# Dilated attention: tokens ordered by class mod 4, eight blocks a head in equal halves

## What is computed

```python
DIL_GROUPS = ((128, 1), (512, 4), (2048, 16))     # (window, dilation r)
# query t attends t - j*r, j = 0..window/r
s = einsum(q_g, k_g) * 64 ** -0.5                 # masked outside that window
m = max(s); p = exp(s - m); den = sum(p)
o_g = (p @ v_g) / den;  lse_g = m + log(den)
o = sum over g of softmax(lse)_g * o_g            # then o @ w_o, added to x
```

## Time and profile before

| | before |
|---|---|
| median of 3 runs | 2204.69 us (2204.66 to 2206.47) |
| the profiled execution | 2205.75 us |
| its span | 2203.9 us |
| TensorE busy | 2168.8 us, 98% |
| VectorE busy | 1475.0 us, 67% |
| ScalarE busy | 1196.1 us, 54% |
| GpSimd busy | 217.0 us, 10% |
| dilated stage, from its first product to the end of y | about 1719 to 2021 us of the span |
| between the last product of n = 8 and the first of y | 1934.9 to 1998.8 us |

### The profile page before, as it was taken

One profiled execution on the slowest core, in us unless ns is written; L12 is line 12 of the kernel. 1 busy time (PEld: TensorE's weight loads), 2 busy tenths in 40 slices (PEclk: granted clock), 3 DMA queues, 4 the chain that ended last, 5 costly groups with the idle time before them and its releaser, 6 DMA issues.

```text
span 2203.9 us, 29727 instructions
## 1 busy us (share of the span) xinstructions
PE 2168.8 (98%) x11759; PEld 1837.7 (83%) x11759; DVE 1475.0 (67%) x2097; ACT 1196.1 (54%) x1814; POOL 217.0 (10%) x228
## 2 busy tenths in 40 slices
PE   9999999999999999999999999998999999999999
PEld 9878888997888878888877888777888888877887
DVE  7645755897666767667745755686655699685665
ACT  5555544756445645455555544566544566475443
POOL 0000100472000011000000200002000100051000
PEclk9999999999999999999999999999999999999999
DMA  8534656523655535655544655551655566513653
GB/s 267 187 134 153 203 192 191 163 77 120 208 190 165 174 115 190 192 191 173 185 145 160 172 190 194 182 173 58 206 191 191 182 173 187 172 39 102 201 191 119
DMA packets 201817, 368.95 MB, mean 167 GB/s; under 512 B 6991, under 2 KB 142543, under 8 KB 201680
## 3 DMA queue, kind: packets, MB, share of 16 engines
q1 hardware_dynamic: 198064, 358.70, 49.7%
q0 software_dynamic: 3616, 8.35, 2.2%
HBM read 365.97 MB, written 1.05 MB: 167 GB/s over the span
## 4 chain that ended last, share of the span: by engine, by line
PE 90%; DVE 6%; ACT 2%; POOL 1%; issue 1%; DMA 0%; ACTq 0%; DVEq 0%; POOLq 0%
PE PS L680 48%; PE PS L811 14%; PE PS L813 7%; PE PS L799 6%; PE PS L849 2%; PE PS L1008 2%; PE PS L929 1%; DVE wlo L2048 1%; PE PS L856 1%; PE PS L1099 1%; POOL wlo L2976 1%; ACT whi L1463 1%; PE PS L1363 1%; PE PS L916 1%; DVE st L2874 1%
## 5 line engine op out<-in xcount | busy, mean ns | idle before, releaser
L2048 DVE TENSOR_TENSOR wlo<-raw,whi 128x1024 fp32r<-128x1024 f32 x658 | 790.4, 1228 | 183.8 <-ACT whi L1463 182.8
L1463 ACT ACTIVATE whi<-raw 128x1024 fp32r<-128x1024 f32 x680 | 700.0, 1054 | 367.2 <-PE PS L680 311.6
L680 PE MATMUL PS<-whi,U 128*128 128x512 f32 x1728 | 483.7, 396 | 6.5 <-DVE U L2085 1.4
L680 PEld LDWEIGHTS PS<-whi,U 128*128 128x128 f32 x1728 | 321.4, 188 | 80.8 <-issue 13.5
L811 PE MATMUL PS<-U,whi 128*128 128x512 f32 x1344 | 334.4, 391 | 0.0
L811 PEld LDWEIGHTS PS<-U,whi 128*128 128x128 f32 x1344 | 246.6, 188 | 47.5
L2172 DVE TENSOR_TENSOR AR<-PS,AR 128x512 f32<-128x512 f32 x96 | 66.2, 690 | 303.2 <-ACT AR L1549 303.2
L680 PE MATMUL PS<-wlo,U 128*128 128x512 f32 x864 | 267.7, 391 | 0.0
L680 PE MATMUL PS<-whi,fH 128*128 128x512 f32 x824 | 256.7, 393 | 0.9 <-DVE fL L2310 0.9
L680 PE MATMUL PS<-wlo,fH 128*128 128x512 f32 x824 | 254.4, 390 | 0.0
L680 PE MATMUL PS<-whi,fL 128*128 128x512 f32 x824 | 254.2, 390 | 0.0
(11 more groups left out here) (340 smaller groups left out, 2268.5 us busy)
## 6 DMA issues: line engine op xcount, KB each, us to landing
raw<-in_mlp_w_up SPq DMA_DIRECT2D x64, 1024.0 KB, 5.5
raw<-in_mlp_w_down SPq DMA_DIRECT2D x64, 1024.0 KB, 4.8
raw<-in_ret_w_in SPq DMA_DIRECT2D x48, 1024.0 KB, 5.2
raw<-in_m_w_up SPq DMA_DIRECT2D x32, 1024.0 KB, 5.5
raw<-in_m_w_down SPq DMA_DIRECT2D x32, 1024.0 KB, 4.8
raw<-in_kv_w SPq DMA_DIRECT2D x24, 1024.0 KB, 5.1
raw<-in_ret_w_out SPq DMA_DIRECT2D x16, 1024.0 KB, 4.7
raw<-in_gla_w_in SPq DMA_DIRECT2D x12, 1024.0 KB, 5.0
```

The costliest lines, as they stand in the source:

```text
L680: mm = e.matmul(bank(b + nb), a, w[:, nb * 512:(nb + 1) * 512], start=(begins and n < 2), stop=(ends and n >= 4))
L1463: e.activation(split_half(whi, i, x), raw_halves(i)[x], ACT.Copy).then_inc(HI.tick((i, x)), 1)
L2048: e.tensor_tensor(split_half(wlo, i, x), raw_halves(i)[x], split_half(whi, i, x).bitcast(F32), ALU.subtract).then_inc(LO.tick((i, x)), 1)
```

## The change

Tokens of the queries, keys and values are put in the order "class mod 4 is 0 or 1" (128 tokens), then "2 or 3" (128). A half then holds whole classes. Group 0 (dilation 1) still needs both halves of the keys for each half of the queries, two blocks of 128x128; groups 1 and 2 need only the block of their own half. So every unit has four blocks a head: 512 columns, and there are 16 equal units i = 2j + a in place of 8 large and 8 small ones. In columns per pair of heads: 2 x (768 + 384) = 2304 before, 2 x 2 x 512 = 2048 now.

The order is made where data is transposed anyway: the transposes of the queries (turn_heads with by_class) and of the keys' and values' input (turn_quarter) write their columns to permuted places in PSUM; the values products write back to the natural order. Because a transposed column block now spreads over both halves of U, the first keys product waits for both token tiles of the split input and not for one (fresh_u). The inverse root of each token is permuted for the keys and values by four small products (turn_r) and a copy; rotation tables for keys and values come permuted from memory (ct_kv).

The steps change as follows. A unit's scores take a bank for each head, and two units fit in banks 4 to 7, so scores wait for the mask of the unit two earlier. Mask and maximum are one instruction per head (tensor_tensor_reduce, which negates; the exponential then has scale -1). All scalings are on VectorE, one head at a time; GpSimd has none. Four buffers hold probabilities (before two for each size) and two hold their transposes. The value products alternate between banks 2 and 3. Scores of units 0 to 3 stand after the four chunks of the last values product; in the loop scores run four units ahead, and each values step comes one unit after its transposes. y begins with the second token tile, and the last values step stands between the two tiles. The two halves of a weight chunk of y are split inside the loop, at units 13 and 14.

Only the new side is shown, since the old one stands above; "..." marks where lines are left out.

```diff
@@ place_dil @@
+            p.ct_kv = take(2, 2, 64)
+            p.order = take(128)
             Arena.at = base - 256
...
+            p.prb = [take(2, 512) for _ in range(2)] + [xn[:, n, :].rearrange("p (c n) -> p c n", c=2) for n in range(2)]
+            p.masks = side[:, 0:1024].rearrange("p (a n) -> p a n", a=2)
+            p.pT = [take(1024), side[:, 1024:2048]]
@@ the transposes of the shared keys' and values' input, and the wait before its products @@
+                    by_class = PS[:, o:o + 128].rearrange("p (a m r) -> p m a r", a=2, r=2)
+                    tr = e.transpose(by_class, src[:, tt, k * 128:(k + 1) * 128], ident[:, :])
...
+                return lambda k, tt: [UL[t, tt, k // 2] if t[1] == "in" else UL[t, 1, k // 4]]
@@ turn_heads, for the queries @@
+                            if by_class:
+                                to = PS[:, o:o + 256].rearrange("p (a t m r) -> p t m a r", a=2, t=2, r=2)[:, tt, :, :, :]
@@ pe_dil @@
+                def turn_r():
+                    e.wait_ge(*R[S])
+                    e.wait_ge(*UL[(S, "in"), 1, 0])
+                    e.wait_ge(*s_dil_mask[2])
+                    for a in range(2):
+                        for tt in range(2):
+                            mm = e.matmul(PS[64 * tt:64 * tt + 64, 2048 + a:2049 + a], p.order[:, 64 * a:64 * a + 64],
+                                          st[:, 4 + tt:5 + tt], start=True, stop=True, skip_group_check=True)
+                    mm.then_inc(LRK.tick("turned"), 1)
...
+                    if n == 8:
+                        scores(c)
+                def scores(i):
+                    j, a = divmod(i, 2)
+                    e.wait_ge(*(MAXED[S, i - 2, 1] if i >= 2 else HTC[S, 5, 3]))
                     for g in range(3):
                         for c in range(2):
...
+                            po, o = 64 * c, (4 + 2 * a + c) * 512
+                            if g == 0:
+                                out, keys = PS[:, o:o + 256], p.kT[0][po:po + 64, j, :]
+                            else:
+                                out, keys = PS[:, o + 128 + 128 * g:o + 256 + 128 * g], p.kT[g][po:po + 64, j, 128 * a:128 * a + 128]
+                            mm = e.matmul(out, p.q_all[po:po + 64, g, j, 128 * a:128 * a + 128], keys, start=True, stop=True)
+                    mm.then_inc(SCORE.tick((S, i)), 1)
+                def turn(i):
+                    e.wait_ge(*(PCOPY[S, i - 1] if i else LV[2, 0]))
                     for c in range(2):
...
+                        e.wait_ge(*LPR[i, c])
+                        for n in range(4):
+                            o = c * 512 + n * 128
+                            tr = e.transpose(PS[:, o:o + 128], p.prb[i % 4][:, c, n * 128:n * 128 + 128], ident[:, :])
+                    tr.then_inc(PTURN.tick((S, i)), 1)
+                def values(i):
+                    j, a = divmod(i, 2)
+                    o = l_value_bank(j) * 512
+                    e.wait_ge(*PCOPY[S, i])
+                    if a == 0:
+                        e.wait_ge(*(LV[2, 1] if j < 2 else LOL[j - 2] if j < 7 else MAXED[S, 15, 1]))
+                    blocks = [(0, 0, 0), (0, 1, 128), (1, a, 256), (2, a, 384)]
+                    for n, (g, s, m) in enumerate(blocks):
                         for c in range(2):
...
+                            po = 64 * c
+                            out = PS[po:po + 64, o:o + 256].rearrange("p (m a r) -> p a m r", a=2, r=2)[:, a, :, :]
+                            probs = p.pT[i % 2][:, c * 512 + m:c * 512 + m + 128].rearrange("p (m r) -> p m r", r=2)
+                            mm = e.matmul(out, p.v[g][:, s, j * 128 + po:j * 128 + po + 64], probs,
+                                          start=(n == 0), stop=(n == 3), skip_group_check=True)
+                    mm.then_inc(VALUE.tick((S, i)), 1)
...
+                for i in range(16):
+                    turn(i)
+                    if i < 12:
+                        scores(i + 4)
+                    if i:
+                        values(i - 1)
                 gemm_a((S, "y"), c0 + 36, 4, u_ap, (0, 2), fresh=lambda k, tt: [LOL[k]],
...
+                       free=([PCOPY[S, 15]], [LOL[5], LOL[6]]), ends=False, entry=lambda: values(15), rows=(1, 0))
                 gemm_last(S, lambda k, tt: u_ap(4 + k, tt), lambda k, tt: [LOL[k + 4]])
@@ act_dil @@
+                def exps(i):
+                    sm = p.prb[i % 4]
                     for c in range(2):
...
+                        at = 128 + 2 * (i % 4) + c
+                        e.wait_ge(*MAXED[S, i, c])
+                        e.activation(sm[:, c, :], sm[:, c, :], ACT.Exp, scale=-1.0, bias=st[:, at:at + 1],
+                                     accum_out=st[:, at + 8:at + 9]).then_inc(EXPED.tick((S, i, c)), 1)
+                def turned(i):
+                    e.wait_ge(*PTURN[S, i])
+                    if i >= 2:
+                        e.wait_ge(*VALUE[S, i - 2])
+                    e.activation(p.pT[i % 2], PS[:, 0:1024], ACT.Copy).then_inc(PCOPY.tick((S, i)), 1)
                 def output(j):
                     o = l_value_bank(j) * 512
...
+                    e.wait_ge(*VALUE[S, 2 * j + 1])
...
+                hi_of(c0 + 32, 2)
+                exps(0)
+                hi_of(c0 + 34, 1)
+                exps(1)
+                hi_of(c0 + 35, 1)
+                read_v(2, 0)
+                exps(2)
+                read_v(2, 1)
+                exps(3)
+                for i in range(16):
+                    turned(i)
+                    if i < 12:
+                        exps(i + 4)
+                    if i >= 2 and i % 2 == 0:
+                        output(i // 2 - 1)
+                    if i in (13, 14):
+                        hi_half()
+                output(7)
@@ dve_dil @@
+                def mask(i):
+                    e.wait_ge(*SCORE[S, i])
+                    if i >= 4:
+                        e.wait_ge(*PTURN[S, i - 4])
+                    for c in range(2):
+                        at = 128 + 2 * (i % 4) + c
+                        e.tensor_tensor_reduce(p.prb[i % 4][:, c, :], bank(4 + 2 * (i % 2) + c), p.masks[:, i % 2, :], -1.0, 3.0e38,
+                                               ALU.add, ALU.min, st[:, at:at + 1]).then_inc(MAXED.tick((S, i, c)), 1)
+                def scaled(i):
+                    for c in range(2):
+                        at, sm = 136 + 2 * (i % 4) + c, p.prb[i % 4][:, c, :]
+                        e.wait_ge(*EXPED[S, i, c])
+                        own(e.reciprocal(st[:, at + 8:at + 9], st[:, at:at + 1]))
                         settle()
...
+                        e.tensor_scalar(sm, sm, st[:, at + 8:at + 9], None, ALU.mult).then_inc(LPR.tick((i, c)), 1)
...
+                    if n == 1:
+                        e.wait_ge(*LRK["turned"])
+                        e.tensor_copy(st[:, 6:8], PS[:, 2048:2050]).then_inc(LRK.tick("copied"), 1)
...
+                lo_of(c0 + 32, 1)
+                e.wait_ge(*s_dil_mask[2])
+                mask(0)
+                lo_of(c0 + 33, 1)
+                scaled(0)
+                mask(1)
+                lo_of(c0 + 34, 1)
+                scaled(1)
+                mask(2)
+                lo_of(c0 + 35, 1)
+                scaled(2)
+                mask(3)
+                for i in range(16):
+                    if i < 12:
+                        mask(i + 4)
+                    if i < 13:
+                        scaled(i + 3)
+                    if i >= 2 and i % 2 == 0:
+                        output(i // 2 - 1)
+                    if i in (13, 14):
+                        lo_half()
+                output(7)
@@ pool_dil @@
@@ constants @@
+    order = np.concatenate([t[t % 4 < 2], t[t % 4 >= 2]])
+    c["rope2_kv"] = np.ascontiguousarray(c["rope2"][:, order, :])
+    c["by_class"] = np.ascontiguousarray(c["ident"][:, order[order < 128]])
     full = []
     for r in (1, 4, 16):
...
+        dist = order[:, None] - order[None, :]
         full.append(np.where((dist >= 0) & (dist % r == 0) & (dist // r <= 128), 0.0, -1e30))
...
+    c["dilm"] = np.stack([np.concatenate([full[0][s], full[1][s, s], full[2][s, s]], 1)
+                          for s in (slice(0, 128), slice(128, 256))]).astype(np.float32)
```

More of the change, by code:

```diff
@@ L661, in l_value_bank @@
         def l_value_bank(j):
-            return 3 if j < 7 else 7
-        LRC = Event(sem("s_dil_sum_r"), l_rows)
-        LPR = Event(sem("s_dil_probs"), [k + (c,) for k in l_rows if k[1] for c in range(2)])
+            return 2 + j % 2 if j < 7 else 6
+        LRK = Event(sem("s_dil_r"), ["turned", "copied"])
+        LPR = Event(sem("s_dil_probs"), [(i, c) for i in range(16) for c in range(2)])
         LOH = Event(sem("s_dil_o_hi"), range(8))
@@ L1365, in scores @@
-                    mm.then_inc(SCORE.tick((S, j, u)), 1)
-                def turn(j, u):
-                    pp, w = p.prb[u][j % 2], 384 + 384 * u
-                    if (j, u) == (0, 1):
```

(49 more changed lines are left out.)

139 lines of the change are left out of this document (27 added, 112 removed).

## The result

The changed kernel takes 2193.39 us (median of 4 runs, 2192.64 to 2194.41) and the kernel before, beside it on the same chip, 2205.12 us (4 runs, 2204.66 to 2206.47): ratio 0.9949, 95% interval 0.9936 to 0.9961. A second set of 5 runs gave 2193.42 us and 0.9947 (0.9934 to 0.9961). The forecast was 2192.7 us.

What follows compares the result with a forecast made beforehand. VectorE bound the old kernel, TensorE close behind; TensorE was to bound the new at 3.12 us a unit. Last n = 8 chunk to y: 63.96 to 50.5 us, 13.5 less; minus 1.05 and 0.4, net 12.0: 2192.7 us, range 2186 to 2200.

Steps and rivals of the forecast that it cites:

- turn(0) to turn(1): Start of the attention units: unit 0's copy stands behind unit 3's exponentials, 3.6 us from one turn to the next.
- units 12 to 14: End of the attention, no scores left: turn, copy and turn follow each other, 2.44 us three times and 0.1, 7.4 us.
- keys' wait and inverse roots: Outside the stretch: first keys product waits 1.05 us more for splits, permuting inverse roots costs TensorE 0.4 us.
- The sum of 4.65: From the last n = 8 chunk's end to turn 1: scores, masks, exponential, copy and hand-overs, 4.65 us; less 1.05 gives 3.6.
- The 0.28 us from ScalarE's copy to the turn: Delay from the end of ScalarE's copy to the TensorE turn waiting for it, 0.28 us, counted in the loops.
- The loop over the engines: Turn, scores, masks, exponential, copy, next turn: 5.5 us in two units, 2.75 a unit, 2.94 with an output, below 3.12.
- 1 (TensorE lighter than counted): Units 1 to 11: TensorE needs less, VectorE and ScalarE set 2.6 us a unit; 5.7 less, 2187 us; chance 0.12.
- 2: Units 1 to 11: the loop through the engines sets the pace, 3.4 us a unit; 3 more, 2196 us; chance 0.20.
- rival 4: Values and transposes writing PSUM with a step take twice the time: 19.6 us more, 2212 us; chance 0.07.
- rival 3: Units 12 to 15: TensorE's clock falls, four turns take about 0.75 us more each; 3 us, 2196; chance 0.06.
- Rival 5: Units stay near VectorE's old 3.6 us, as fused masks or one-head scalings cost more; 2200 us and above; chance 0.05.
- GpSimd's 4.59 us: GpSimd's scalings on the chain at the attention's end before the change, 4.59 us; forecast to go with GpSimd's scalings.

## Why the prediction was right

The mechanism is the one forecast: units 1 to 11 became TensorE's, at 3.12 us forecast and 3.12 measured, with VectorE at 2.6. That the two agree to the hundredth is luck: the loads of the scores take 0.96 and not 0.89, and one of the three gaps is 0.12 and not 0.17, and the two errors cancel. Term by term, in us:

| step | predicted | measured |
|---|---|---|
| more scores inside n = 8 | +0.87 | 42.03 - 40.95 = +1.08 |
| scores of unit 3 | 1.05 | 1.10 |
| turn(0) to turn(1) | 3.6 | 1941.27 - 1938.03 = 3.24 |
| units 1 to 11 | 34.3 | 1975.64 - 1941.27 = 34.37 |
| units 12 to 14 | 7.4 | 1982.37 - 1975.64 = 6.73 |
| unit 15's turn, values 14 | 2.06 | 2.12 |
| values 15 inside y | 1.2 | 21.88 - 20.64 = 1.24 |
| sum, against 63.96 | 50.5 | 49.88 |
| keys' wait and inverse roots | +1.45 | +0.97 |
| net in the span | -12.0 | -13.1 |

The first row is from the start of n = 8 to the end of its last chunk (1894.90 to 1936.93 after, 1893.92 to 1934.87 before). The scores in it are 3 x 1.08 - 2.37 = 0.87 more, as forecast; the other 0.2 is in the products. The medians differ by 11.7, the spans by 13.1: the profiled execution before was 0.6 above its median, the one after 0.8 below. So the forecast of 12.0 is 1.1 too small against the spans it was worked out for, and its nearness to the medians' 11.7 is in part luck too. The sum of 4.65 in the prediction is 4.63 by its own terms.

Three terms were mis-sized: turn(0) to turn(1) and units 12 to 14 with one cause, and the time added elsewhere.

- **The 0.28 us from ScalarE's copy to the turn.** I read 1957.87 to 1958.15 in the earlier trace rows as the way from ScalarE to TensorE. The trace after has 0.04: the copy ends at 1977.91 as the chain has it, and the turn begins at 1977.96. The rest in the earlier trace rows was TensorE's own work: its scores of 256 columns began at 1956.66, and six of them with the hand-over take 1.50, which ends at 1958.16. So a loop of the tail is 2.20 us and not 2.44 (three times 0.24 is the 0.7), and it is 0.24 of the 0.36 by which turn(0) to turn(1) is shorter. The other 0.1 is what is left of errors that cancel: the scores' end costs 0.02 and not 0.24, mask and exponentials 2.25 and not 2.04, the copy 0.92 and not 1.02.
- **The keys' wait and the inverse roots do not add.** Each was sized well: the inverse roots cost TensorE 0.55 us (0.4 forecast; it was 0.08 ahead of before when it came to them and 0.47 behind after them), the later splits about 1.0 (1.05 forecast). VectorE ended its eight splits at the same time as before (starts 1790.93 and 1790.99), as it hangs on its own earlier work, not on TensorE. TensorE came to the wait 0.48 later (1792.19, before 1792.21 - 0.50 = 1791.71), from the inverse roots, and that lateness vanished in the wait: the product goes on at 1793.18, when all eight splits are done (1790.93 + 2.15 = 1793.08), 0.97 after the 1792.21 of before. The larger of two delays that meet in one wait counts, not their sum.

The loop over the engines was put at 2.75 a unit, 2.94 with an output; the run with half the values shows 2.85 when it sets the pace. Of the rivals, 1 (TensorE lighter than counted) fell: its loads stand back to back. So did 2: the loop is as short as forecast, and does not set the pace of 3.12. Only in the tail, units 12 to 14, does a loop, the one through ScalarE's copy, set it, as the sum had it. Strided writes (rival 4) cost nothing: 0.053 against 0.054 us an instruction for the values, and the 16 transposes of the keys' input take 1.75 us with the step as without. No clock fell (rival 3): 1.00 in both windows, though half of TensorE's work in the tail is transposes. The Trainium skill ("TensorE: Matmul & The Clock Gate", Part 4: PE-mode transpose) says that such transposes do not count as activity for the clock in the way other products do; no fall from that is to be seen here. That the clock can fall in this stage is shown by two other runs: the kernel before (0.76 at its end) and the run with mask and maximum apart (0.83 around a wait of 2.48 us). Rival 5 needed VectorE at 3.6 us a unit. It stands at 2.6; the run with mask and maximum apart, at 4.02, shows the whole gain gone.

GpSimd's 4.59 us left the chain, as forecast, but I gave the wrong reason: the fused mask alone takes them off it, with the scalings still on GpSimd, and one of a unit's two scalings put back there costs nothing. The 63.96 us of before also held 1.6 us of a lower clock at the end, which the sum took in unseen.

What I gave no thought to is the order on VectorE: the gain would have been 3.8 us smaller with two lines exchanged. I had worked out VectorE's sum, 2.6 us, which is the same in both orders. And the splits in units 13 and 14, which I gave nothing, hold 1.0 us that an earlier y would have lost: right in the sum against before, but only with them. Not tested each by itself are the order by class, the scores four units ahead and the alternating banks of the values; the runs show only what they bring together.

## What to carry to other kernels

Work out the busy time of each engine for one period and take the largest, but then write down each queue in order and ask of every instruction whether something ready stands behind it: that alone was a third of this gain. When two changes each lift a different bound, test them apart: here the fused mask gave 4.1 us, all the rest none, both together 11.7. Delays that end in one wait are a maximum; only what follows the last of them on the path adds.

## What the runs showed of the hardware

- A product that writes PSUM with a step of its columns costs as one without (0.053 and 0.054 us for each values instruction of 128 columns; 1.75 us for 16 transposes of the keys' input, both before and after).
- From the end of ScalarE's copy in the chain to TensorE's next phase it is 0.04 us; where nothing is waited for, 0.12 to 0.17 us still lie between the weight loads of two of TensorE's phases, three times in a unit of 3.12 us.
- The fused mask and minimum of 512 columns takes 0.69 us and the next starts 0.61 to 0.62 later, where add and maximum apart take 1.3 to 1.4 us a head (1950.59 to 1952.00 and on to 1953.32). The fused instruction is as long as the add alone, 0.69.
- GpSimd's scaling of 128 x 512 takes 1.56 us (12.52 us for 8), VectorE's 0.49.
